# Expert loop: up biases as a broadcast row added by VectorE instead of two bias products

## The reference

```python
def expert_block(args):
    xe, e = args
    gate = jnp.minimum(xe @ w_gate[e] + b_gate[e], SWIGLU_LIMIT)
    up = jnp.clip(xe @ w_up[e] + b_up[e], -SWIGLU_LIMIT, SWIGLU_LIMIT)
    act = (up + 1) * (gate * jax.nn.sigmoid(SWIGLU_ALPHA * gate))
    return act @ w_down[e] + b_down[e]
```

## Time and profile before

| what | value |
|---|---|
| median of 3 runs | 2948.45 us (2945.43 to 2949.97) |
| span of the profiled execution | 2949.2 us, 41378 instructions |
| TensorE (PE) busy | 2878.5 us, 98% |
| VectorE (DVE) busy | 2014.6 us, 68% |
| ScalarE (ACT) busy | 1602.4 us, 54% |
| POOL busy | 549.8 us, 19% |
| moved by DMA | 638.87 MB, mean 217 GB/s |
| granted TensorE clock, mean | 0.991 |

### The profile page before, as it was taken

The page is one execution under the profiler, slowest core; times in us unless marked ns, Lnnn a source line. Parts: engine busy times, 40 slices in busy tenths (PEclk is TensorE's granted clock), DMA queues, the critical chain, the costliest instruction groups (busy, mean ns, idle before and its releaser), DMA issues.

```text
span 2949.2 us, 41378 instructions
## 1 busy us (share of the span) xinstructions
PE 2878.5 (98%) x14988; PEld 2301.8 (78%) x14988; DVE 2014.6 (68%) x2262; ACT 1602.4 (54%) x1749; POOL 549.8 (19%) x479
## 2 busy tenths in 40 slices
PE   8999999998999999999999899999999999999999
PEld 4687888765788888877777688888888888888887
DVE  8551233578621236836763699999999999999998
ACT  5242223336522224434532577777777777777775
POOL 1002100013112100003100132322222222222231
PEclk9899999998999999999999999999999999999999
DMA  8322322221032232110022699999999999999995
GB/s 350 145 100 93 120 88 86 90 74 44 26 132 86 100 114 93 58 72 1 1 86 86 220 413 384 381 384 388 386 386 386 387 386 385 381 385 382 382 382 221
DMA packets 88924, 638.87 MB, mean 217 GB/s; under 512 B 10449, under 2 KB 11665, under 8 KB 26097
## 3 DMA queue, kind: packets, MB, share of 16 engines
q1 hardware_dynamic: 78592, 599.97, 52.0%
q0 software_dynamic: 9936, 36.75, 4.6%
q10 hardware_dynamic: 288, 0.65, 0.1%
HBM read 611.28 MB, written 26.05 MB: 216 GB/s over the span
## 4 chain that ended last, share of the span: by engine, by line
PE 51%; DVE 3%; POOL 1%; issue 1%; ACT 0%; SPq 0%; DMA 0%; DVEq 0%; ACTq 0%
PE banks L263 15%; PE banks L265 15%; PE banks L264 15%; PE banks L2177 1%; PE banks L3355 1%; PE banks L3215 1%; PE banks L3337 1%; PE banks L2166 1%; DVE stat L2319 1%; PE banks L2193 1%; DVE arena_rounded L3234 1%; DVE arena L2332 0%; POOL arena L2373 0%; PE banks L3321 0%; DMA arena_rounded<-bias_dram 0%
## 5 line engine op out<-in xcount | busy, mean ns | idle before, releaser
L3234 DVE TENSOR_TENSOR arena_rounded<-arena,arena_rounded 128x2048 fp32r<-128x2048 f32 x420 | 950.7, 2285 | 89.2 <-ACT arena_rounded L3230 89.2
L3230 ACT ACTIVATE arena_rounded<-arena 128x2048 fp32r<-128x2048 f32 x420 | 801.8, 1918 | 207.5 <-PE banks L265 132.8
L263 PE MATMUL banks<-arena_rounded,operand_rounded 128*128 128x512 f32 (+1 forms) x2064 | 817.6, 396 | 3.3 <-DVE small_rounded L3526 1.3
L264 PE MATMUL banks<-arena_rounded,operand_rounded 128*128 128x512 f32 (+1 forms) x2064 | 801.9, 389 | 0.0
L265 PE MATMUL banks<-arena_rounded,operand_rounded 128*128 128x512 f32 (+1 forms) x1504 | 583.3, 388 | 0.0
L263 PEld LDWEIGHTS banks<-arena_rounded,operand_rounded 128*128 128x128 f32 x2064 | 387.9, 188 | 83.9 <-issue 4.5
L264 PEld LDWEIGHTS banks<-arena_rounded,operand_rounded 128*128 128x128 f32 x2064 | 388.3, 188 | 76.5 <-issue 1.0
L265 PEld LDWEIGHTS banks<-arena_rounded,operand_rounded 128*128 128x128 f32 x1504 | 282.5, 188 | 58.7
L263 PE MATMUL banks<-operand_rounded,arena_rounded 128*128 128x512 f32 (+2 forms) x712 | 267.5, 376 | 5.3 <-PE banks L265 5.2
L264 PE MATMUL banks<-arena_rounded,arena_rounded 128*128 128x512 f32 (+1 forms) x688 | 266.8, 388 | 0.0
L265 PE MATMUL banks<-operand_rounded,arena_rounded 128*128 128x512 f32 (+2 forms) x712 | 263.9, 371 | 0.0
(11 more groups left out here) (519 smaller groups left out, 3876.7 us busy)
## 6 DMA issues: line engine op xcount, KB each, us to landing
arena<-in_gate SPq DMA_DIRECT2D x140, 1024.0 KB, 7.7
arena<-in_up SPq DMA_DIRECT2D x140, 1024.0 KB, 7.8
arena<-in_down SPq DMA_DIRECT2D x140, 1024.0 KB, 5.8
arena<-in_dense SPq DMA_DIRECT2D x62, 2048.0 KB, 7.7
arena<-in_dense SPq DMA_DIRECT2D x6, 1024.0 KB, 5.6
small<-in_rows SPq DMA_DIRECT2D x7, 512.0 KB, 8.1
resid<-in_x SPq DMA_DIRECT2D x4, 512.0 KB, 8.2
expert_sums<-operand SPq DMA_DIRECT2D x4, 512.0 KB, 4.4
```

Source lines behind the costliest of these rows:

```text
L263: nc.tensor.matmul(out, left[0], right[0], start=start, stop=False)
L264: nc.tensor.matmul(out, left[0], right[1], start=False, stop=False)
L3230: nc.scalar.activation(high[q % NHI], raw[:, q, :], ACT.Copy).then_inc(high_ready, 1)
L3234: nc.vector.tensor_tensor(low[q], raw[:, q, :], high[q % NHI].bitcast(F32), ALU.subtract).then_inc(low_ready, 1)
```

## The change

The up biases no longer go through TensorE. A new DRAM tensor `up_rows_dram` (32 x 1024) takes `b_up + 1` of every expert, straight from `bias_raw`. For each block a DMA reads the row of its expert and sends it to all 128 partitions, into `up_wide`, the half of `e["bias"]` that held the up columns. For block 0 ScalarE issues it, once the down biases are made; for later blocks SP does, after the load of piece 8, and after VectorE's two adds of the block before. VectorE's `hide` adds the row to the bank into `e["up"]`, and clips `e["up"]` in place. In `open_products` the bias product stays for the two gate halves. In `route`, SP writes `up_rows_dram` first of the bias DMAs; POOL waits for its landing before it makes `bias_low`, and SP waits for it at the end.

```diff
--- before.py
+++ after.py
@@ -2684,6 +2684,8 @@
     e["spread"], e["spread_again"] = (e["spread_twice"][:, :, n * NE:(n + 1) * NE] for n in range(2))
     e["tokens_dram"] = k.nc.dram_tensor("tokens_dram", (S, D + NE), F32, kind="Internal").ap()
     e["bias_dram"] = k.nc.dram_tensor("bias_dram", (2, 3, NE, D), F32, kind="Internal").ap()
+    e["up_rows_dram"] = k.nc.dram_tensor("up_rows_dram", (NE, D), F32, kind="Internal").ap()
+    e["up_wide"] = e["bias"][:, D:2 * D].bitcast(F32)
     e["bias_in"] = k.nc.alloc_semaphore(name="expert_biases_in")
     e["in"] = [k.nc.alloc_semaphore(name=f"expert_weights_in_{n}") for n in range(PIECES)]
     return e
@@ -2748,6 +2750,8 @@
     def sync(sp):
         split_of = lambda h: e["bias_dram"][h].rearrange("r e (q c) -> (e q) r c", c=QD)
         of_role = lambda part: part.rearrange("p (r c) -> p r c", c=QD)
+        sp.wait_ge(bias_up, 1)
+        sp.dma_start(e["up_rows_dram"].rearrange("e (q c) -> (e q) c", c=QD), e["bias_raw"][:, QD:2 * QD]).then_inc(bias_up, 16)
         sp.wait_ge(bias_high, 1)
         sp.dma_start(split_of(0), of_role(e["bias_high"].bitcast(F32))).then_inc(bias_out, 16)
         sp.wait_ge(bias_low, 1)
@@ -2766,6 +2770,7 @@
         for q in range(SOON, EARLY):
             load_expert_piece(k, e, sp, q, 0)
         sp.wait_ge(rows_out, 16 * (ST + 1))
+        sp.wait_ge(bias_up, 1 + 16)
 
     def bias_entry(act):
         act.wait_ge(bias_up, 1)
@@ -2961,6 +2966,7 @@
         nc.gpsimd.memset(e["bias"][3 * NE:, D:2 * D].bitcast(F32), 0.0).then_inc(bias_zero, 1)
         pool.wait_ge(bias_high, 1)
         pool.wait_ge(bias_zero, 1)
+        pool.wait_ge(bias_up, 1 + 16)
         nc.gpsimd.tensor_tensor(e["bias_low"], e["bias_raw"], e["bias_high"].bitcast(F32), ALU.subtract).then_inc(bias_low, 1)
         pool.wait_ge(fed["added"], ST)
         pool.wait_ge(bias_low, 1)
@@ -3181,6 +3187,7 @@
      added) = (k.sem(f"last_{n}") for n in names)
     names = ("biased", "biases_act", "biases_dve", "sums_out", "turned", "high_ready")
     biased, biases_act, biases_dve, sums_out, first_turned, first_high = (k.sem(f"first_{n}") for n in names)
+    wide_in, up_added = (k.sem(f"bias_{n}") for n in ("wide_in", "up_added"))
     sums_in = [k.sem(f"last_sums_in_{t}") for t in range(ST)]
 
     GATE_TOP = LIMIT / (1.0 + math.exp(-ALPHA * LIMIT))
@@ -3203,6 +3210,11 @@
     def block_number(engine, turn):
         return nc.s_assert_within(engine.snap(turn), 0, NBLK - 2,
                                   skip_runtime_bounds_check_because="only turns below the last block come here")
+
+    up_wide = e["up_wide"]
+
+    def load_wide(engine, expert):
+        engine.dma_start(up_wide, e["up_rows_dram"][expert].partition_broadcast(P)).then_inc(wide_in, 16)
 
     def gather_rows(pool):
         pool.indirect_dma_start(e["x_rows"], None, e["tokens_dram"],
@@ -3252,6 +3264,9 @@
 
                         sp.wait_ge(used, PIECES * b + (q + 2 - PIECES))
                         load_expert_piece(k, e, sp, q, expert)
+                        if q == 8:
+                            sp.wait_ge(up_added, 2 * b)
+                            load_wide(sp, expert)
             sp.wait_ge(last_staged, 4)
             for t in range(ST):
                 sp.dma_start(sums[:, t, :], k.sums_dram[t * P:(t + 1) * P, :]).then_inc(sums_in[t], 16)
@@ -3347,8 +3362,9 @@
                 for j in range(4):
                     d = 4 * (q % 2) + j
                     x = [t[:, d * P:(d + 1) * P] for t in (e["x_high"], e["x_low"])]
-                    i = exact_product(nc, k.psum[:, r, :], x, (w[0][:, j, :], w[1][:, j, :]), start=(d == 0), stop=False)
-                if q % 2 == 1:
+                    i = exact_product(nc, k.psum[:, r, :], x, (w[0][:, j, :], w[1][:, j, :]), start=(d == 0),
+                                      stop=(d == DT - 1 and r % 2 == 1))
+                if q % 2 == 1 and r % 2 == 0:
                     if q == 1:
                         pe.wait_ge(chosen, b + 1)
                     at = (r % 2) * D + (r // 2) * NB
@@ -3437,6 +3453,8 @@
             for t in range(ST):
                 act.wait_ge(biased, 2 * t + 1)
                 nc.scalar.activation(half(first_rows[t], 0), k.psum[:, first_bank(0, t), :], ACT.Copy).then_inc(biases_act, 1)
+            act.wait_ge(biased, 2 * ST)
+            load_wide(act, 0)
             act.wait_ge(first_turned, 1)
             nc.scalar.activation(half(e["x_high"], 0), half(x_banks, 0), ACT.Copy).then_inc(first_high, 1)
             act.wait_ge(x_turned, 1)
@@ -3515,7 +3533,11 @@
             def hide(b, h):
 
                 dve.wait_ge(used, during(b, 4 * h + 4))
-                V.tensor_scalar(half(e["up"], h), k.psum[:, 2 * h + 1, :], 1.0 + LIMIT, 1.0 - LIMIT, ALU.min, ALU.max).then_inc(clipped, 1)
+                if h == 0:
+                    dve.wait_ge(wide_in, 16 * b + 16)
+                V.tensor_tensor(half(e["up"], h), k.psum[:, 2 * h + 1, :], half(up_wide, h), ALU.add).then_inc(up_added, 1)
+                dve.wait_ge(up_added, 2 * b + h + 1)
+                V.tensor_scalar(half(e["up"], h), half(e["up"], h), 1.0 + LIMIT, 1.0 - LIMIT, ALU.min, ALU.max).then_inc(clipped, 1)
                 dve.wait_ge(gated, 2 * b + h + 1)
                 dve.wait_ge(clipped, 2 * b + h + 1)
                 V.scalar_tensor_tensor(out=half(e["gate"], h), in0=half(e["gate"], h), scalar=GATE_TOP, in1=half(e["up"], h),
```

## The result

The changed kernel takes 2961.15 us (median of 9 runs, 2958.14 to 2969.50) against 2947.52 us of the kernel before (9 runs, 2943.35 to 2955.37). The ratio is 1.0044, 95% interval 1.0031 to 1.0056: slower by 13.0 us, 9.1 to 16.5. The forecast was slower, by 24.7 us, 2973.2 us within 2959 to 2990.

What follows compares the result with a forecast made beforehand. TensorE, busy 98%, was taken to bound the kernel, with VectorE's cycle binding after the change. +18.4 us (loop), +1.1 (last block) and +5.2 (POOL's wait) gave +24.7 on 2948.45: 2973.2 us, range 2959 to 2990.

Steps and rivals of the forecast that it cites:

- the way of VectorE's cycle: Expert loop: VectorE's added work sets the period, giving 2973 us, range 2960 to 2991; chance 0.76.
- POOL's new wait: Ahead of the loop: POOL waits for the up-row write queued behind 6 MB of pieces; +5.2 us, all reaching the end.
- TensorE's saving: Loop: two bias products fewer per block, 0.46 us; TensorE's bound falls from 35.49 to 35.03 us.
- d, the cost per half: VectorE in each hidden half: new add plus shorter clip, less the old clip; net 0.54 us, bounds 0.42 and 0.79.
- VectorE's cycle today: Loop before the change: dependence path through TensorE, ScalarE and VectorE back to x_low; 34.95 us, 0.54 under the period.
- The period: Time per block in the loop: 34.95 + 2 x 0.54 = 36.03 us, +0.54 us per block.
- Where TensorE would wait: Each block: ahead of turn_hidden of the second half, about 0.6 us, and at the first piece, on x_low.
- The last block: End of the loop: TensorE already waits on take_hidden_low, so both halves' added VectorE cost lands there; +1.1 us.
- The row transfer costs nothing: SP's queue in the loop: 512 KB more per block stays hidden, cost 0; if queues bind instead, 1.2 us per block.
- ScalarE's row 0 costs nothing: Ahead of the loop: load_wide on ScalarE sits in an idle stretch before the first x_high; cost 0.
- The clock ahead of the loop: Before the loop: a longer TensorE pause could hold its clock at half speed for longer; not priced.

Runs made afterwards that it cites:

- the clip doubled: Changed kernel with each half's clip done twice on VectorE, same result: 2990.6 us, ratio 1.0143 against the kernel before.
- the order changed: Changed kernel with VectorE's second-half hide, take_hidden_low and take_x_low moved ahead of less urgent take_low work: 2936.1 us, 0.9965 against the kernel before.
- route part alone: Kernel before plus only the up-row write to DRAM and the POOL and SP waits on it, old loop: 2951.7 us, ratio 1.0016.
- rows not sent: Changed kernel without the row transfers of blocks 1 to 34, block 0's row added in every block: 2961.8 us, 1.0045 against the kernel before.
- rows early: Changed kernel with SP writing up rows to DRAM before its projection wait and six weight pieces: 2958.3 us, 1.0030 against the kernel before.
- the two with the new order: Changed kernel with VectorE's urgent results moved earlier, 2936.1 us; the same plus up rows written before the six weight pieces, 2933.0 us.
- all three repairs: Changed kernel with VectorE reordered, up rows written early, and block 0's row sent after the down bias rows landed: 2930.9 us, 0.9944 against before.

## Why the prediction was right, and where it was too large

The forecast said slower, by the way of VectorE's cycle and POOL's new wait. Both are shown: the first by the rows left out (no change), the clip doubled (+0.78) and the order changed (-0.72 per block); the second by the early rows and by the route part alone. The time, 13 us more, is about half of the 24.7 forecast. It would have been further off, had not a loss of 3.5 us in block 0, which the forecast didn't have, made up for what it had too much ahead of the loop and in the last block (1.5 and 0.7). By its steps:

- **TensorE's saving**, 0.46 us per block: 0.48 measured. That it was swallowed by VectorE: right.
- **d, the cost per half**, 0.54: the start-to-start times are 0.72 (add) and 0.53 (clip) against 0.79 for the old clip, so 0.46. The durations were right, 683 and 427 ns; what I had too large was the gap behind the add, 0.11 assumed and 0.04 measured.
- **VectorE's cycle today**, 34.95: too long by 0.15. I took VectorE's printed idle time of 0.50 us off, but its instructions overlap by 0.08 (2218.24 + 6.69 = 2224.93, and the next starts at 2224.85; the same in the kernel before), so the gap between starts was 0.57. And the sigmoid follows the first load by 6.01 us instead of 6.09: before, TensorE was still busy when it loaded, and the product started 0.22 us behind its load (2225.18); now it starts 0.05 behind (2238.70).
- **The period**: with those numbers 6.01 + 2.44 + (2238.53 - 2211.38 = 27.15) + 0.12 = 35.72. These stretches follow one another round one block, so they add up to its period whatever binds; what counts is that in none of them an engine waits for anything but the one before it in the cycle. The forecast 36.03 was 0.31 over: 2 x 0.08 from d, 0.07 and 0.08 from the cycle. This is the step that failed in size. A difference of two nearly equal lengths, +0.54 by forecast and +0.24 by measurement, doubles when one of them is off by one per cent. 34 times 0.31 is 10.5 of the 11.7 us that the forecast is over. The rows of before would have given the overlap, had I read starts instead of idle times.
- **Where TensorE would wait**: at `turn_hidden` of half 1 about 0.6 us (0.60) and at `x_low` (0.21): right. A third wait, for `take_hidden_low` (0.19), was not in the forecast.
- **The last block**, +1.1: 0.4.
- **The row transfer costs nothing**: right in the loop. The page "DMA: Bandwidth & Descriptors" of the Trainium skill, section "Where 436 GB/s comes from", has HBM transfers held at some 358 GB/s. No run here shows that limit: the loop moved 384 GB/s before and 408 with two rows per block (448.31 MB from 1760 to 2860 us).
- **POOL's wait**, +5.2: the DMA landed 18.0 us after T0, where I had 18.6; shares +4.65, SP's first token DMA 5.1 later (18.77 to 23.90 from T0), first product on the biases (L3336, "first expert product" in the forecast) +4.14, first product of block 0 +3.66. I had let the whole delay through. SP caught up 0.6 on its next DMAs, and the bias loads landed 0.4 sooner behind their issue.
- **ScalarE's row 0 costs nothing**: wrong. It was free on ScalarE, and cost 1 to 2 us on the queues, beside stores for which ScalarE waits. The prediction priced the issue and not the transfer.
- **The clock ahead of the loop**, left without a price: the forecast feared a longer stretch at half speed. The 16 products on the biases took 6.49 us at a granted clock of 0.57 before, mostly at the lower of the two levels (1.2 GHz), and 5.53 at 0.69 after, so that stretch was shorter. But it differs between profiles of the same code: "rows not sent", the same up to there, had 3.93 us at 1.00, all at 2.4 GHz.

Block 0's 3.5 us are better read together with the way to it, since one gives what the other takes. From T0 to block 0's `x_low` the kernel before took 75.45 us and the changed one 82.63, 7.2 more. By pairs of profiles that differ in one step, POOL's wait is 4.5 to 4.6 of it (after and "rows early", before and "route part alone", the two with the new order), row 0 beside the stores 1.2 and 1.8, and the old order of VectorE 0.9 and 1.0: 6.6 to 7.4 in all. The kernel with all three repairs is back at 75.33. Finer than that it can't be split: kernels that differ in nothing that should count here lie up to 0.6 us apart (82.63 and 83.18 with and without the later rows), and the 34.2 for block 0 of the kernel before is the lowest of the four profiles whose loop is its own or differs in one edit (the others have 34.7, 35.2 and 35.3).

## What to carry to other kernels

An engine that is busy 93% of a block (VectorE had 2.5 us of gaps in 35.49) has no spare 7% if its results are due in the middle: measure the length of the cycle that runs through it, from starts and not from busy or idle times, and compare it with the period; what is added to it counts from the margin on. When work is taken off the engine that binds, look for the next cycles first and change the order of the other engine so that what is due soonest goes first: here that alone turned a loss of 13 us into a gain of 10, and the two repairs ahead of the loop made it 14 to 16. And look at what stands on a queue ahead of a new DMA: the 128 KB write landed 14.8 us after its issue behind 6 MB of loads and 1.7 us with nothing of them ahead, so a write whose landing someone needs goes first.

## What was unexpected of the hardware

- A VectorE instruction that waits for the one before it starts 0.04 us after the add's end (0.683 us, next start 0.72 later), but 0.10 after a single clip (0.427, next start 0.53), and only 0.03 to 0.04 after each of two clips in a row (0.46, 0.47). I can't say why the single clip has the longer gap.
- One more row per block shows in the landing times far more than in the period: 7.7, then 18.0 us for a down piece, with 0.07 us per block lost.
- The stages before T0, the same in all the kernels but for one small DMA, took from 1645.07 to 1654.66 us, and that goes with the granted clock between 100 and 150 us: 0.79 to 0.82 in the four profiles with T0 at 1651.42 or later, 0.98 to 1.00 in the ten others (1648.81 or sooner). The two executions with T0 over 1654 are 8.4 and 9.5 us longer than the median of their kernel (2969.5 against 2961.15, 2942.5 against 2932.99), so this is much of the spread between executions, and the reason to compare profiles by distances from a mark behind it.
